# Weight parts of a hybrid decoder layer stored column by column from two blocks in turn

## The reference, cut to what matters

```python
h = einsum('btd,dn->btn', rmsnorm(x, ln_g), w_in)     # w_in: 4096 x 13472, split into q, k, v, gates, indexer, pool input
o_a = sparse attention over the best keys by an indexer score; o_b = multi-scale pooling
mix = concat([o_a * silu(g_a), o_b * silu(g_b)])
y   = rmsnorm(x + einsum('btm,md->btd', mix, w_out))  # w_out: 4096 x 4096
```

## Time and profile before

| | |
|---|---|
| median of 3 runs | 2083.04 us (2082.86 to 2083.18) |
| span of the profiled execution | 2081.8 us; the page gives no other time of it, and the median lies 1.2 us above the span |
| PE busy | 2067.9 us (99% of the span) |
| PE weight loads (PEld) | 1973.7 us (95%) |
| DVE busy | 1288.9 us (62%) |
| ACT busy | 735.1 us (35%) |
| POOL busy | 406.3 us (20%) |
| mean DMA rate | 195 GB/s |
| granted TensorE clock | 0.998 of full speed over the span |

### The profile page before, as it was taken

The page is one execution under the profiler, slowest core; times in us unless marked ns, Lnnn a source line. Parts: engine busy times, 40 slices in busy tenths (PEclk is TensorE's granted clock), DMA queues, the critical chain, the costliest instruction groups (busy, mean ns, idle before and its releaser), DMA issues. The chain is left out here.

```text
span 2081.8 us, 38884 instructions
## 1 busy us (share of the span) xinstructions
PE 2067.9 (99%) x14191; PEld 1973.7 (95%) x14191; DVE 1288.9 (62%) x1747; ACT 735.1 (35%) x917; POOL 406.3 (20%) x574
## 2 busy tenths in 40 slices
PE   9999999999999999999999999999999999999998
PEld 7888888999999999999999999999999999999998
DVE  5545545578687445666776767565565866555664
ACT  6433333322222333333333323333334433333333
POOL 1100000021210010235642103222222511111100
PEclk9999999999999999999999999999999999999999
DMA  8777777755554565665666657878877855555554
GB/s 234 208 220 214 222 211 203 212 167 159 157 160 140 179 192 171 176 195 174 195 201 201 178 153 231 242 245 260 248 248 246 258 170 169 164 164 165 157 167 147
DMA packets 341330, 406.03 MB, mean 195 GB/s; under 512 B 20332, under 2 KB 316204, under 8 KB 341000
## 3 DMA queue, kind: packets, MB, share of 16 engines
q1 hardware_dynamic: 293704, 291.75, 47.6%
q0 software_dynamic: 29968, 94.61, 14.7%
q10 hardware_dynamic: 17584, 18.70, 2.7%
HBM read 377.68 MB, written 31.45 MB: 197 GB/s over the span
## 5 line engine op out<-in xcount | busy, mean ns | idle before, releaser
L246 DVE TENSOR_TENSOR lo<-raw,hi 128x1024 fp32r<-128x1024 f32 x542 | 694.5, 1285 | 566.6 <-ACT hi L241 565.2
L270 PE MATMUL main<-XX,hi 128*128 128x320 f32 x3264 | 1030.1, 316 | 0.2 <-DVE XX L1655 0.2
L272 PE MATMUL main<-XX,lo 128*128 128x320 f32 x3264 | 1009.5, 309 | 0.0
L271 PE MATMUL main<-XX,hi 128*128 128x320 f32 x3264 | 1009.0, 309 | 0.0
L241 ACT ACTIVATE hi<-raw 128x1024 fp32r<-128x1024 f32 x542 | 569.8, 1057 | 854.7 <-PE main L272 540.6
L270 PEld LDWEIGHTS main<-XX,hi 128*128 128x128 f32 x3264 | 613.2, 188 | 9.0 <-issue 5.0
L271 PEld LDWEIGHTS main<-XX,hi 128*128 128x128 f32 x3264 | 613.3, 188 | 2.3
L272 PEld LDWEIGHTS main<-XX,lo 128*128 128x128 f32 x3264 | 612.7, 188 | 0.0
L257 PE MATMUL main<-XX,hi 128*128 128x512 f32 x1024 | 355.9, 392 | 0.0
L258 PE MATMUL main<-XX,lo 128*128 128x256 f32 x1024 | 287.0, 280 | 0.0
L257 PEld LDWEIGHTS main<-XX,hi 128*128 128x128 f32 x1024 | 191.6, 187 | 42.4 <-issue 0.2
(11 more groups left out here) (304 smaller groups left out, 1544.8 us busy)
## 6 DMA issues: line engine op xcount, KB each, us to landing
raw<-w_in SPq DMA_DIRECT2D x416, 512.0 KB, 3.9
raw<-w_out SPq DMA_DIRECT2D x128, 512.0 KB, 3.7
deck<-cache_k POOLq DMA_DIRECT2D x64, 256.0 KB, 4.4
projT<-stg ACTq DMA_DIRECT2D x35, 320.0 KB, 2.9
keep<-cache_v POOLq DMA_DIRECT2D x40, 256.0 KB, 3.4
deck<-cache_v POOLq DMA_DIRECT2D x24, 256.0 KB, 3.6
deck<-maskD POOLq DMA_DIRECT2D x8, 516.0 KB, 5.6
ipg<-cache_idx_k POOLq DMA_DIRECT2D x64, 64.0 KB, 3.1
```

The source lines that it names most:

```text
L246: nc.vector.tensor_tensor(low, raw[:, slot, :, 0:width], high.bitcast(F32), ALU.subtract).then_inc(lo_ready, 1)
L270: nc.tensor.matmul(sums, wh, XH[:, k, :], start=first, stop=False)
L271: nc.tensor.matmul(sums, wh, XL[:, k, :], start=False, stop=False)
L272: mm = nc.tensor.matmul(sums, wl, XH[:, k, :], start=False, stop=last)
```

## The change

The `raw` chunk still comes in as it was. ACT and DVE now write `hi` and `lo` with their columns in another order: column c of block 0, column c of block 1, column c + 1 of block 0, and so on. `by_block` is the view [4, 2 blocks, 128] of a slot stored so, and its last axis has a step of two elements (8 bytes). So ACT's output, DVE's output and DVE's second input have a step of two, and the stationary operands of L257, L258 and L270 to L272 are read with that step. In `set_products` the moving operand is two runs of 128 with a step of two. The number of instructions, their sizes, the semaphores and the slots stay.

```diff
+        def by_block(w):
+
+            return w.rearrange("p k (c n) -> p k n c", n=2)
...
-            dst = hi[:, slot, :, 0:width] if home is None else home
-            nc.scalar.activation(dst, raw[:, slot, :, 0:width], ACT.Copy).then_inc(hi_ready, 1)
+            dst = hi[:, slot, :, :] if home is None else home
+            nc.scalar.activation(by_block(dst), raw[:, slot, :, :].rearrange("p k (n c) -> p k n c", n=2),
+                                 ACT.Copy).then_inc(hi_ready, 1)
...
-            high, low = homes or (hi[:, slot, :, 0:width], lo[:, slot, :, 0:width])
-            nc.vector.tensor_tensor(low, raw[:, slot, :, 0:width], high.bitcast(F32), ALU.subtract).then_inc(lo_ready, 1)
+            high, low = homes or (hi[:, slot, :, :], lo[:, slot, :, :])
+            nc.vector.tensor_tensor(by_block(low), raw[:, slot, :, :].rearrange("p k (n c) -> p k n c", n=2),
+                                    by_block(high.bitcast(F32)), ALU.subtract).then_inc(lo_ready, 1)
...
-                    wh, wl = (w[:, slot, kk, n * P:n * P + P] for w in (hi, lo))
+                    wh, wl = (by_block(w[:, slot, :, :])[:, kk, n, :] for w in (hi, lo))
...
-                    wh, wl = (w[:, slot, kk, cols[n]:cols[n] + P] for w in (hi, lo))
+                    wh, wl = (by_block(w[:, slot, :, :])[:, kk, n, :] for w in (hi, lo))
...
-                    wh, wl = (w[:, kk, :] for w in weights[m])
-                    sums = SETS[i][0:r, 0:HB]
+                    wh, wl = (by_block(w)[:, kk, :, :] for w in weights[m])
+                    sums = SETS[i][0:r, 0:HB].rearrange("p (n c) -> p n c", n=2)
```

More of the change, by code:

```diff
@@ L234, in load_segment, with hi_chunk @@
             quad(n - 1, False, True)
-        def hi_chunk(act, c, slot, uses, width=2 * P, guard=True, home=None):
+        def hi_chunk(act, c, slot, uses, guard=True, home=None):
             act.wait_ge(raw_in[slot], uses)
@@ L239, in hi_chunk, with lo_chunk @@
                 act.wait_ge(chunk_used, c - (SLOTS - 1))
-            dst = hi[:, slot, :, 0:width] if home is None else home
-            nc.scalar.activation(dst, raw[:, slot, :, 0:width], ACT.Copy).then_inc(hi_ready, 1)
-        def lo_chunk(dve, c, slot, width=2 * P, homes=None):
+            dst = hi[:, slot, :, :] if home is None else home
+            nc.scalar.activation(by_block(dst), raw[:, slot, :, :].rearrange("p k (n c) -> p k n c", n=2),
+                                 ACT.Copy).then_inc(hi_ready, 1)
+        def lo_chunk(dve, c, slot, homes=None):
             dve.wait_ge(hi_ready, c + 1)
-            high, low = homes or (hi[:, slot, :, 0:width], lo[:, slot, :, 0:width])
-            nc.vector.tensor_tensor(low, raw[:, slot, :, 0:width], high.bitcast(F32), ALU.subtract).then_inc(lo_ready, 1)
+            high, low = homes or (hi[:, slot, :, :], lo[:, slot, :, :])
+            nc.vector.tensor_tensor(by_block(low), raw[:, slot, :, :].rearrange("p k (n c) -> p k n c", n=2),
+                                    by_block(high.bitcast(F32)), ALU.subtract).then_inc(lo_ready, 1)
         def paired(pe, c, slot, j, banks):
@@ L259, in paired, with products @@
             mm.then_inc(chunk_used, 1)
-        def products(pe, c, slot, j, banks, cols, rot=0):
+        def products(pe, c, slot, j, banks, rot=0):
             pe.wait_ge(lo_ready, c + 1)
@@ L287, in pe_quad @@
                 else:
-                    products(*at_, (0, P), rot)
+                    products(*at_, rot)
                 if weave:
```

## The result

The kernel after takes 2116.02 us (median of 4 runs, 2115.78 to 2116.12) against 2083.09 us before (4 runs): ratio 1.0158, 95% interval 1.0146 to 1.017. It is slower by 33 us, 1.6%; 1955 was predicted, and faster. The profiled execution took 2115.78 us with a span of 2114.2.

The account below looks back on a forecast made before the run. It took PE's number of matmuls times their start-to-start distance as the bound. Span 2081.8 - 135 + 5 = 1952 us, plus 1.2 outside it, gave 1953; it predicted 1955, with an 8-in-10 range of 1935 to 2246.

Parts of the forecast that it names:

- Part 1: Main-loop matmuls L257, L258, L270 to L272: stepped stationary loads match the moving stream's pace, overhead falls, 135 us gained.
- Part 2: 288 matmuls of set_products, moving operand now stepped: no change taken; bounds 28 us more and 3 us less.
- Part 3: ACT writes hi with a step: even doubled to 2.1 us for a chunk, nothing on the path.
- Part 4: DVE reads hi and writes lo with a step: 1.23 us unchanged; upper bound 2.45 us, 53 us late at most.
- Part 5: Raw DMAs: a faster PE asks for chunks sooner; 13 us lost if 260 GB/s were the ceiling, 5 taken.
- (c): PE's distances stay, being no matter of memory: 2083 us, up to 28 more by set_products, 16 by DVE; chance 0.16.
- (a): Stationary loads: overhead counts memory places touched, so the step doubles it; 135 us more, 2218, or 2246; chance 0.17.
- (b): Stepped stationary loads go at half pace, 228 ns for each main matmul; 907 us more, 2990; chance 0.09.

Follow-up runs that it names:

- e6: The kernel before, with L270 to L272 loading only 64 of each block's 128 stationary columns, the other half of each product left out; 2075.07 us.
- e8: The kernel before with the tiles XX, hi, lo and late in bfloat16 in place of fp32r; 1962.02 us, ratio to before 0.9414.
- e10: The kernel after with those tiles in bfloat16 and columns of four blocks stored in turn, a step of four elements (8 bytes); 2247.15 us.
- e3: The kernel after, but set_products reads its moving columns without step and DVE takes the step reading the sums from PSUM; 2084.16 us, ratio to before 1.0003.
- e9: The kernel after with the tiles XX, hi, lo and late in bfloat16, so a step of two elements is 4 bytes; 1966.63 us.

## Why the prediction was wrong

- **What bounds the kernel** was right: PE's distances from start to start set the time, before and after.
- **Part 1, the step of the stationary operands, failed**, by the whole of its 135 us. It said that overhead comes from two streams that pass over memory at unequal pace, and ends when both run alike. The distances stayed at 147 and 346.7 ns, although the stepped loads (195 ns) walked over twice the bytes in nearly the same time. e6 took away the ground: half the columns loaded leave 146.4 ns. I had set 113.7 against 120.0 ns and read "half the columns, half the overhead" from one pair of rows, with 256 moving columns; at 320 columns it does not hold. Why it does at 256, where the distance falls by 6.3 ns, stays open. The other ground, plain float32 matmuls without the overhead, differed in format as well as in pace. e8 shows that the format alone takes the overhead down, at the same pace: 2.8 ns in bfloat16. In the kernel after, the moving stream of `set_products` at half pace still has 226.7 - 213.3 = 13.4 ns. But e10's bfloat16 stream at the same step of 8 bytes has 14.6 (227.9 - 213.3) where it had 2.3 without a step, so these need not be the 13.3 ns of fp32r. Whether it is the load or the moving stream of fp32r that costs the 13.3 ns stays open; no run had the one without the other.
- **Part 2, `set_products`, was mis-sized in the choice**: "I take no change" stood for what came out at the upper bound, 28 us; measured 31.4. The bound came from the pace of plain float32 with its 1.6 ns; over the same pace the stepped stream had 13.4 ns. With no row for a stepped moving operand I should have kept the middle at least.
- **Part 3, ACT**, was right that nothing shows: 92 ns more for a chunk, not the doubling allowed for, and hidden.
- **Part 4, DVE**, was right: 1285 ns before and after. The two pages of the Trainium skill can now be told apart. "Advanced Engine Details and Errata", SBUF Cachelines (two hits on a line of 16 bytes for full speed), fits DVE and nearly ACT for 4-byte elements: step 2 costs 0 and 92 ns, step 4 takes both to 2.08 us. It also fits the stationary operand of fp32r. It doesn't fit the moving operand, which is at half pace at step 2 already, nor e10, whose 2-byte elements 8 bytes apart also give two hits on each line and cost 2.55 us. By the hop prices of "Vector Engine (DVE) Microarchitecture Reference", 5.2, the estimate was 2.0 us at a step of two; the trace has 1.29, and comes to 2.08 at a step of four only.
- **Part 5, DMA**, was not put to the test by this change. e8, 6% faster, moved 284 GB/s in one slice, so 260 was no ceiling.
- **The rivals.** (c), no gain and up to 28 us of loss by part 2, is what happened, and its 2083 + 28 = 2111 is 5 us short of 2116; I gave it 0.16. The rule of the Trainium skill, "TensorE: Matmul & The Clock Gate", Part 2, behind it (a load takes no read bandwidth from the running matmul) agrees with e6, where half the load gave back 0.8 ns of 13.3. The opposite direction is another matter: beside the stepped stream the loads grew from 192 to 207 ns. That 2116 lies between 1935 and 2246 is no merit of the forecast: the upper end came from (a), a mechanism that did not occur. (a) and (b) did not occur at step 2; (b)'s 228 ns for each main matmul is close to what step 4 brought.

## What to carry to other kernels

The elements of the operand that streams through the array should lie next to each other: 8 bytes from element to element cost half its pace, in fp32r and in bfloat16. With 4-byte elements the stationary operand, DVE's operands (and ACT's nearly) take a step of 8 bytes for nothing and pay at 16. If a layout forces the step on someone, the read of the result from PSUM took it for nothing in e3. And before a gain is built on an overhead, ask in which single respect the rows with and without it differ: here two respects had changed at once, and the one not looked at, the format, moved the overhead in e8 by itself.

## What the runs showed that I had not expected

- The step of an fp32r stationary operand is free at 8 bytes and makes the load 135 ns longer at 16 (195 to 330 ns).
- Writes of 2-byte elements with a step are dearer than of 4-byte ones at the same distance: 8 bytes apart, 2548 (ACT) and 2552 ns (DVE, which also reads one such input) against 1149 and 1285 for 1024 elements. At 4 bytes apart (e9) they already cost 1354 and 1420, against 1054 and 1293 without a step (e8).
- A stepped moving operand is not slower at step 8 than at step 2 (218.7 and 226.7 ns).
- A bfloat16 stationary operand with a step of 8 bytes is loaded in 115 ns instead of 98 (e10 and e8), with the main loops still at 136 ns.
